# The memory's query as turned segments at the head of the gate stage, and attention's last group at one item per unit

## What is computed

```python
h = rmsnorm(x, norm1_g)
z = h @ w_in                       # split into the parts below
qa, ka, va                         # 3 groups x 8 heads x 64: windowed attention, dilations 1, 4, 16
qm, km, vm                         # memory: 8 heads, 64 (q, k) and 128 (v) wide
om, gif, ga, gb                    # gates
qm = qm * 64 ** -0.5
o_att = combine(attention of the 3 groups)
h_m   = mlstm(qm, km, vm, gates)   # in chunks, with a running state
mixed = sigmoid(ga) * (o_att @ w_att_out) + sigmoid(gb) * ((sigmoid(om) * h_m) @ w_m_out)
x = x + mixed @ w_o
y = x + swiglu(rmsnorm(x, norm2_g))
```

## Time and profile before

| | us |
|---|---|
| median of 3 runs | 2161.61 (2161.17 to 2162.16) |
| the profiled execution | 2158.37 |
| its span, first to last instruction | 2156.6 |
| TensorE busy (share) | 2117.9 (98%) |
| VectorE busy | 1066.8 (49%) |
| ScalarE busy | 631.7 (29%) |
| GpSimd busy | 715.7 (33%) |
| mean granted clock of TensorE, share of full | 0.998 |

### The profile page before, as it was taken

The page is one execution under the profiler, slowest core; times in us unless marked ns, Lnnn a source line. Parts: engine busy times, 40 slices in busy tenths (PEclk is TensorE's granted clock), DMA queues, the critical chain, the costliest instruction groups (busy, mean ns, idle before and its releaser), DMA issues.

```text
span 2156.6 us, 36189 instructions
## 1 busy us (share of the span) xinstructions
PE 2117.9 (98%) x14248; PEld 1977.4 (92%) x14248; DVE 1066.8 (49%) x2112; ACT 631.7 (29%) x1354; POOL 715.7 (33%) x636
## 2 busy tenths in 40 slices
PE   7999999999999999999999999999999999999999
PEld 6788899999877778999989999999999999999998
DVE  5675777775233341233266544398454454442212
ACT  5221465544233232333211011143332332221001
POOL 3433321232112222222052334224544544554310
PEclk9999999999999999999999999999999999999999
DMA  6625534355548834545467641415545545387712
GB/s 201 210 101 170 176 117 144 131 187 174 180 154 286 271 132 149 165 148 162 134 214 239 207 154 54 148 60 180 183 150 178 182 151 178 105 329 288 259 41 79
DMA packets 233735, 365.17 MB, mean 169 GB/s; under 512 B 39222, under 2 KB 134262, under 8 KB 230870
## 3 DMA queue, kind: packets, MB, share of 16 engines
q1 hardware_dynamic: 211534, 317.48, 44.3%
q10 hardware_dynamic: 22032, 45.38, 6.1%
HBM read 276.19 MB, written 174.68 MB: 209 GB/s over the span
## 4 chain that ended last, share of the span: by engine, by line
PE 52%; DVE 5%; issue 2%; DMA 1%; ACT 1%; SPq 0%; DVEq 0%; ACTq 0%
PE ps L2855 20%; PE ps L2199 17%; PE ps L366 4%; PE ps L367 4%; PE ps L368 4%; PE ps L1637 1%; DMA h_mem<-c_ht 1%; DVE acc L3126 1%; PE ps L1412 0%; DVE x_a L2549 0%; PE ps L1629 0%; PE ps L1620 0%; PE ps L1646 0%; DVE x_c L2549 0%; DVE misc L3102 0%
## 5 line engine op out<-in xcount | busy, mean ns | idle before, releaser
L341 POOL CAST whi<-raw 128x512 fp32r<-128x512 f32 x228 | 167.6, 735 | 1046.1 <-PE ps L682 431.0
L343 POOL TENSOR_TENSOR wlo<-raw,whi 128x512 fp32r<-128x512 f32 x231 | 323.3, 1400 | 34.6 <-issue 10.3
L366 PE MATMUL ps<-whi,x_a 128*128 128x512 f32 x416 | 178.6, 429 | 0.0
L736 ACT ACTIVATE zt<-ps 128x512 f32<-128x512 f32 x104 | 62.1, 597 | 356.6 <-PE ps L368 302.6
L367 PE MATMUL ps<-wlo,x_a 128*128 128x512 f32 x416 | 166.5, 400 | 0.0
L368 PE MATMUL ps<-whi,x_a 128*128 128x512 f32 x416 | 166.5, 400 | 0.0
L366 PE MATMUL ps<-whi,x_b 128*128 128x512 f32 x416 | 166.0, 399 | 0.0
L368 PE MATMUL ps<-whi,x_b 128*128 128x512 f32 x416 | 166.0, 399 | 0.0
L367 PE MATMUL ps<-wlo,x_b 128*128 128x512 f32 x416 | 165.9, 399 | 0.0
L2855 PE MATMUL ps<-x_a,whi 128*128 128x258 f32 x960 | 156.2, 285 | 2.0 <-DVE acc L2657 1.8
L2855 PE MATMUL ps<-x_c,whi 128*128 128x258 f32 x960 | 154.5, 283 | 0.5 <-DVE acc L3334 0.5
(11 more groups left out here) (416 smaller groups left out, 4930.1 us busy)
## 6 DMA issues: line engine op xcount, KB each, us to landing
out<-in_cache_kv_w SPq DMA_DIRECT2D x144, 512.0 KB, 6.3
raw<-in_w_in SPq DMA_DIRECT2D x147, 256.0 KB, 4.2
a_tr<-tt SPq DMA_DIRECT2D x48, 256.0 KB, 2.0
out<-in_cache_kv_w SPq DMA_DIRECT2D x24, 508.0 KB, 5.5
raw<-in_w_down SPq DMA_DIRECT2D x44, 256.0 KB, 6.0
gates<-e_sg ACTq DMA_DIRECT2D x16, 516.0 KB, 3.8
rw<-gates ACTq DMA_DIRECT2D x16, 516.0 KB, 4.7
out<-zt SPq DMA_DIRECT2D x26, 256.0 KB
```

Of the source, the lines that this page charges most:

```text
L341: pool.tensor_copy(self.whi[:, self.place(p), :], raw).then_inc(self.w_hi, 1)
L343: pool.tensor_tensor(self.wlo[:, self.place(p), :], raw, self.whi[:, self.place(p), :].bitcast(F32), ALU.subtract).then_inc(self.w_lo, 1)
L366: nc.tensor.matmul(out, lhs[0], rhs[0], start=start, stop=False)
L736: act.activation(self.zt[:, u % Z, :], ps[:, u % 2, :], ACT.Copy, scale=self.scale(u)).then_inc(self.ev, 1)
```

## The change

The query leaves the tile kinds: `KINDS` keeps 12 kinds, so the projection stage has 108 units. The weights of the query come first among the gate stage's pieces, and the gate stage has four units (`QUERY`), 12 segments, ahead of the gates. ScalarE takes them with a copy and the scale of 1/8 and issues two stores per unit: the prompt's part, already turned, to `m_tr`, and the new tokens' part, single elements in transposed order, to `zm_s`. The chunks start 12 segments later (`FIRST` = 15). The loads of chunks 0 and 1 move from `sp_init` to segment 13 and wait for all stores of the query.

Attention's groups 0 and 1 keep their units; group 2 starts at the same unit 90 and takes one unit per item. The new tokens' scores start at unit 78 instead of 81; in the code that is three units ahead of the memory's key.

The diff, without the hunks that drop the scale of 1/8 from the tile units:

```diff
@@ -51,7 +51,7 @@
 COPIES = (55, 121)
 MAKE = (1, 2, 4, 7, 5, 6, 3)
 FIRST = 8
-KINDS = [(0, 2), (0, 0), (1, 2), (0, 1), (1, 0), (1, 1), (2, 0), (2, 1), (2, 2)] + [("m", x) for x in range(4)]
+KINDS = [(0, 2), (0, 0), (1, 2), (0, 1), (1, 0), (1, 1), (2, 0), (2, 1), (2, 2)] + [("m", x) for x in range(1, 4)]
 
 
 def bc(ap, shape):
...
@@ -116,7 +116,7 @@
 
     w_in = t["w_in"]
     cols = [x * AW + g * 512 if g != "m" else (CQM, CKM, CVM, CVM + 512)[x] for g, x in KINDS]
-    cols += [CGA, CGA + 512, CGB, CGB + 512, COM, COM + 512]
+    cols += [CQM, CGA, CGA + 512, CGB, CGB + 512, COM, COM + 512]
     out = [[(w_in[k * P:(k + 1) * P, c:c + CW], 0)] for c in cols for k in range(KD)]
     for name, nk in (("w_att_out", 4), ("w_m_out", KD), ("w_o", KD)):
         out += [[(t[name][k * P:(k + 1) * P, c:c + CW], 0)] for c in (0, CW) for k in range(nk)]
...
@@ -635,7 +632,7 @@
         if g == "m":
             if n == NT:
                 return [core.zm_s[:, x * 512:(x + 1) * 512]]
-            return [core.m_tok[n, :, x - 1, :]] if x else []
+            return [core.m_tok[n, :, x - 1, :]]
         if n == NT:
             return [core.z_raw[g, x] if x < 2 else core.z_s[g, 2]]
         out = [core.a_v[g, n]] if x == 2 else []
...
@@ -840,7 +837,8 @@
         self.at, self.exp_marks = {}, {}
         for g in range(G):
             for j in range(self.ITEMS + self.TAIL):
-                self.at[proj.unit(1, 0, 0) + (g * (self.ITEMS + self.TAIL) + j) * 3 // 2] = (g, j)
+                at = g * (self.ITEMS + self.TAIL) + j
+                self.at[proj.unit(1, 0, 0) + (at * 3 // 2 if g < 2 else at + self.ITEMS + self.TAIL)] = (g, j)
         self.loads = {}
         for u, (g, j) in self.at.items():
             if j == 0:
...
@@ -1145,7 +1143,7 @@
         att = Attention(core, proj, c)
         sample = SampleScores(core, proj, c)
         steps = range(proj.steps)
-        late = proj.unit("m", 0, 0)
+        late = proj.unit("m", 1, 0) - 3
         block = c.enter_context(nc.Block())
 
         @block.tensor
...
@@ -1780,8 +1778,6 @@
     def sp_init(self):
         self.core.settle(self.core.nc.sync)
         self.core.nc.sync.wait_ge(self.one, 1)
-        self.load(0)
-        self.load(1)
 
     def store_state(self):
 
...
@@ -2240,11 +2236,11 @@
 
 
     sem, sb, ps = core.sem, core.sb, core.ps
-    U = 2 * KD
-    FIRST, PER, WIDE = 3, 6, 3
-    LOADS = {9: 0, 15: 1, 21: 2}
+    U, QUERY = 2 * KD + 4, 4
+    FIRST, PER, WIDE = 15, 6, 3
+    LOADS = {9: 0, 21: 1, 27: 2}
     p0 = core.taken
-    core.taken += 4 * KD
+    core.taken += 5 * KD
     with ExitStack() as c:
         chunks = Chunks(core, c)
         sg = chunks.sg
...
@@ -2269,11 +2265,21 @@
 
             return p0 + (RING if i < 12 else RING + 8 * (i // 12 - 1) + min(8, i % 12))
 
+        def stored(u):
+
+
+            return 16 * (u // 2) + 16 * min(u // 2, QUERY // 2)
+
         @block.sync
         def _(sp):
             chunks.sp_init()
             for i in range(3 * U):
                 core.load_weights(piece(i))
+                if i == FIRST - 2:
+                    for x in range(2):
+                        sp.wait_ge(out[x], stored(QUERY + x))
+                    chunks.load(0)
+                    chunks.load(1)
                 if step(i) is not None:
                     chunks.sp(step(i))
                 if i in LOADS:
...
@@ -2300,19 +2306,30 @@
         def _(act):
             for i in range(3 * U):
                 u, s = divmod(i, 3)
-                if i == FIRST:
+                if i == 3:
                     core.settle(act)
                 if s == 0 and u >= 2:
-                    act.wait_ge(out[u % 2], 16 * (u // 2))
+                    act.wait_ge(out[u % 2], stored(u))
                 wait_segment(core, act, i, p0, mm)
-                act.activation(sg[:, u % 2, s * SEG:(s + 1) * SEG], ps[:, i % 2, 0:SEG], ACT.Sigmoid).then_inc(ev, 1)
+                part = sg[:, u % 2, s * SEG:(s + 1) * SEG]
+                if u < QUERY:
+                    act.activation(part, ps[:, i % 2, 0:SEG], ACT.Copy, scale=SCALE).then_inc(ev, 1)
+                else:
+                    act.activation(part, ps[:, i % 2, 0:SEG], ACT.Sigmoid).then_inc(ev, 1)
                 if s == 2:
                     act.wait_ge(ev, i + 1)
-                    act.dma_start(core.gates[u], sg[:, u % 2, :]).then_inc(out[u % 2], 16)
+                    if u < QUERY:
+                        act.dma_start(core.m_tr[0, :, :, u * P:(u + 1) * P].rearrange("n p c -> p n c"),
+                                      sg[:, u % 2, 0:S].rearrange("p (n c) -> p n c", n=NT)).then_inc(out[u % 2], 16)
+                        with core.nc.allow_non_contiguous_dma(reason="queries of the new tokens"):
+                            act.dma_start(core.zm_s[:, u * P:(u + 1) * P].rearrange("b c -> c b"),
+                                          sg[:, u % 2, S:T]).then_inc(out[u % 2], 16)
+                    else:
+                        act.dma_start(core.gates[u - QUERY], sg[:, u % 2, :]).then_inc(out[u % 2], 16)
                 if step(i) is not None:
                     chunks.act(step(i))
             for i in range(2):
-                core.defer(out[i], 16 * U // 2)
+                core.defer(out[i], stored(U))
 
         @block.vector
         def _(dve):
```

8 lines of the change are left out of this document (3 added, 5 removed).

## The result

| | before | after |
|---|---|---|
| median of the runs | 2161.89 us (2161.17 to 2163.34, 4 runs) | 2199.26 us (2185.72 to 2206.47, 4 runs) |
| profiled execution | 2158.37 us, span 2156.6 | 2206.47 us, span 2204.7 |
| mean granted clock of TensorE | 0.998 | 0.984 |

The ratio after/before is 1.0164, 95% interval 1.0142 to 1.0186: 37 us slower. Forecast were 2167.6 us with a range of 2157 to 2178. The profiled execution is the longest of the four of after.

The account below looks back on a forecast made before the run. TensorE, busy throughout both stages, was taken as the bound. The terms -52.1 + 45.4 + 4.0 + 1.7 + 5.3 + 1.7 = +6.0 us, put on the median of 2161.61, gave 2167.6 us, range 2157 to 2178.

Parts of the forecast that it names:

- What bounds the kernel: Projection and gate stages: TensorE is busy throughout at full clock, so work removed and waits added count in full.
- Removed and added: Query tile units out of the projection stage, -52.1 us; twelve gate-stage segments in, +45.4 us; direct balance -6.7 us.
- Attention one item per unit: Group 2's attention in the projection stage: an item's 3.6 us chain fits a 5.6 us unit, costed at nothing.
- The tail of the projection stage: Barrier before the gate stage: the new tokens' scores end after the last projection unit, delaying TensorE's restart by +4.0 us.
- E + 6.6: TensorE's predicted restart at the barrier, 6.6 us after the last projection matmul ends; before the change it was 2.65 us.
- the 6 to 7 that I had named as a sign: Expected TensorE idle in us ahead of the gate stage's first matmul, instead of 2.48; near 2.5 would refute the prediction.
- The second rival: Projection stage's end: last score loads and steps run under the last unit, costing nothing; 2155 to 2157 us, chance 0.09.
- The clock after that idle: Start of the gate stage: TensorE's clock falls to 1.2 GHz after the barrier's idle of over 5 us, +1.7 us.
- The first chunk's loads: Gate stage: chunk 0's loads wait for the query's stores, so TensorE stalls +5.3 us, plus +1.7 us for the clock.
- The formula L - 4.7: TensorE's stall in us at chunk 0's scores: landing time of the new tokens' last query store, less 4.7.
- My other end, 4 x 9.6 = 38: Upper bound in us for the element store's landing, if all 9.6 us of a 256-element store is per element.
- The third rival: Gate stage: element stores slower than a query unit's 11.3 us queue up, ScalarE and TensorE wait; 2174 to 2185 us, chance 0.12.

Follow-up runs that it names:

- the part alone: The kernel before with only group 2's attention items put one per unit, the query still a tile kind; ratio 0.9996, 2163.69 us beside 2164.81.
- The earlier scores: The kernel after with the new tokens' query stored as 32-byte rows and their scores started three units earlier; ratio 0.9970, 2159.3 us beside 2166.12.

## Why the prediction was wrong, point by point

**What bounds the kernel** held. The waits put into TensorE's stream came out as time: 38.9 us of waits and the 6.0 us of lower clock behind them make the 40.8 us at chunk 0, together with the balance of the work.

**Removed and added** held. The stage starts 49.4 us earlier, against 52.1 less the tail's 3.7, 48.4. Without the element store, segments from 780.18 to the chunk's scores at 842.86 took 62.7 us, against 16 x 3.78 + 0.2 = 60.7 and 2.0 for the clock.

**Attention one item per unit** costs nothing, shown by the part alone.

**The tail of the projection stage** held. The last projection matmul of after ends at 770.79 + 0.23 = 771.02, TensorE restarts at 777.40, E + 6.4 where I had E + 6.6: +3.7 against +4.0. TensorE's idle time is 5.63 us and not the 6 to 7 that I had named as a sign, because eight matmuls of attention stand behind E (line 946, from 771.12). The chain is the one described. VectorE's and SyncE's timelines:

```profile
772.45 0.67 DVE L1037 COPY ot<-ps 128x512 f32<-128x512 f32 x1
...
775.69 0.68 DVE L1121 TENSOR_TENSOR k_kc<-k_kc,k_qb 8x512 f32<-8x512 f32 x1 [1.26 <-DMA k_qb<-z_s]
776.40 0.67 DVE L1123 TENSOR_REDUCE misc<-k_kc 8x8 f32<-8x512 f32 x1
```
```profile
773.15 0.34 SPq L890 DMA_DIRECT2D o_grp<-ot  x1
773.54 0.32 SPq L1102 DMA_DIRECT2D k_kc<-z_s  x1
773.90 0.29 SPq L1103 DMA_DIRECT2D k_qb<-z_s  x1
```

The store of attention's output, the last pair of loads behind it, VectorE's two operations behind them. The earlier scores took the 3.2 us away again. The second rival (the tail is free) fell.

**The clock after that idle** held in this execution: the first segment takes from 777.40 to 782.70, 5.30 us instead of 3.78, so 1.5 us are lost, against 1.7. That it had to fall is not shown; see the last section.

**The first chunk's loads: here the step failed.** The formula L - 4.7 held. The term that was mis-sized is L, the landing of the element stores: I took 10 us and it measured 25.3 to 35.3, so the stall was 20.8 us and not 5.3. I had taken the row of the 256 element stores as "the same kind of transfer". It is the same in its elements: they lie side by side, from 64 partitions. It is not the same in its rows. The code of that store puts them 512 bytes apart, and the query's store puts them 8192 bytes apart. With rows 512 bytes apart 1024 elements land in 10.4 us, so my 10 was right for that address, and the stride, which I never looked at, is what failed. My other end, 4 x 9.6 = 38, lies near the measured landing by luck: it rests on a price per element, and 1024 elements 64 bytes apart land in 4.3 to 5.0 us. The microsecond of 4 GB/s in the earlier trace rows could not decide either, since stores that land soon show 2 and 5 GB/s as well. One row was read wrongly, without effect on the sum: the median of 6.3 us in the earlier trace rows is over the stores of `h_mem` and the loads that read it back; the eight stores alone have 7.0.

**The third rival is what happened** in its waits, though its reason, that elements are served one by one whatever their address, did not come out: the store takes longer than the 11.3 us of a query unit, ScalarE waits for its buffer and TensorE for ScalarE. I had priced it by the wait at chunk 0 alone, from 12 us on, and the two waits of 18.1 us and the clock behind them were not in its sum; so its 2174 to 2185 us were too low as well, and the range ended at 2178. These two waits are the second part of the failure: the forecast's sum had nothing for them. With the measured terms the sum of the text would be -52.1 + 45.4 + 3.7 + 38.9 + 6.0 + 1.5 = +43.4 us, the last two for the clock up to chunk 0's scores and behind them (3 us at 0.50). That is 2205.0 us on the median, beside the measured 2199.26; the terms are read from the longest of the four runs, 2206.47.

The Trainium skill, DMA: Bandwidth & Descriptors, "Rules for kernel authors", warns of a non-contiguous last dimension, one descriptor per element. Its warning pointed to the right instruction. As a price it doesn't carry: 1024 single elements, by that rule as many descriptors, land in 4.3 to 5.0 us when the elements lie 64 bytes apart. What its "Specifications" say of writes below 512 bytes (a read-modify-write) would fit single elements closer than 64 bytes being slow, but as a price for any small piece it does not fit 32-byte pieces side by side landing in 3.2 us. No run shows a read-modify-write.

## What to carry to other kernels

When a change turns a tile on its way to memory, look at what the small remainder's store becomes: it may be written as single elements side by side from many partitions, and 4 KB then cost more than 512 KB beside them (25 us and more against 3). Store it as it lies (rows of a partition) and turn it at the reader, where TensorE does it in a few transpositions. When you take a landing time from another store's row, compare where both put their elements and rows: count and size alone gave 10 us here and 38 there, and neither for the right reason. And where a term's bounds are 3.5 and 38, carry the far end into the range with its consequences (who waits for the buffer), not into a rival priced by its beginning.

## What the runs showed of the hardware

Single elements of 4 bytes written by one DMA from 128 partitions, 1024 unless said otherwise (medians of four stores): landing in 4.3 and 5.0 us at a distance of 64 bytes, 8.3 us at 16 bytes, 10.4 us side by side in eight rows of 512 bytes, 8.9 us for 128 side by side in one row, 12.9 us for 256 in two rows 8192 bytes apart. In eight rows 8192 bytes apart, 25.3 and 35.3 us are the two landings that the trace has. As 128 pieces of 32 bytes the same data land in 3.2 us.

While such a store is under way, others in the queues are held up: the 512 KB store of the query that was issued at 804.54, 13 us behind the first element store, took 20.2 us, where such stores land in 3.3 us (median of four) without the element stores. The one issued at 847.44 took 4.2.

TensorE's clock is less certain than the sum took it to be. After 2.48 us of idle at the barrier it stayed at 2.4 GHz in the kernel before, and fell to 1.2 GHz in the kernel with the attention part alone, at the same place after the same idle:

```profile
832.00:833.00 1.00, 1.00 (x7) 1.00 (x8) 0.64 (x1) 1.00 (x1) 0.00 (x0) 0.95 0.77 174
833.00:836.00 3.00, 3.00 (x12) 3.00 (x11) 1.63 (x3) 0.14 (x1) 0.00 (x0) 0.50 0.21 69
```

The same is seen behind a wait of 1.09 us at 1127, where the merging of attention begins. The first row is of the kernel before, the second of the kernel without the element store, each after the same 1.09 us:

```profile
1130.00:1135.00 5.00, 5.00 (x52) 4.45 (x51) 4.97 (x9) 0.46 (x1) 3.71 (x4) 1.00 1.05 385
```
```profile
1130.00:1135.00 5.00, 5.00 (x27) 4.66 (x25) 4.62 (x8) 0.46 (x1) 3.39 (x4) 0.76 1.02 387
```

In the kernel after, the same work as before's from 1084 to 1109, and from 1477 to 1502, ran partly at the lower clock (before 1.00 in both):

```profile
1125.00:1150.00 25.00, 25.00 (x161) 24.15 (x161) 15.26 (x31) 3.31 (x6) 13.82 (x13) 0.93 0.56 170
...
1525.00:1550.00 25.00, 22.13 (x173) 21.95 (x172) 19.11 (x23) 9.46 (x17) 18.82 (x13) 0.93 0.75 259
```

That falls of this kind are the 7.3 us which the profiled execution of after lost behind chunk 0 fits what these rows show, 1.8 us each, but no run separates it. The spread of the kernel before over 16 us in the sessions of the experiments goes with the clock: its seven executions with a mean granted clock of 0.998 took 2155.96 to 2159.57 us, its three with 0.991 or 0.992 took 2170.79 to 2172.36. Whoever costs a wait of one to three microseconds should count the fall as a chance, not as a rule.
